# Stick-breaking attention: six projection k-steps moved from the first pair to the last two, and the next pair's sums and root one step later

## The reference

```
qkv = rmsnorm(x) @ w_qkv                 # 1024 x 3072
q, k = rmsnorm(q, q_gain), rmsnorm(k, k_gain)       # per head, over 64
z = q @ k.T / sqrt(64)
log_stay = where(s < t, log_sigmoid(-z), 0)
log_between = reverse_cumsum(log_stay) - log_stay
weights = where(s < t, exp(log_sigmoid(z) + log_between), 0)
x = x + (weights @ v) @ w_o
```

## Time and profile before

| | us |
|---|---|
| median of three runs | 1882.72 |
| the profiled execution's own time | 1882.4 |
| its span | 1880.6 |
| TensorE busy | 1848.2 (98%) |
| VectorE, ScalarE, GpSimd busy | 1034.4, 853.3, 1088.0 |

### The profile page before, as it was taken

The page is one execution under the profiler, slowest core; times in us unless marked ns, Lnnn a source line. Parts: engine busy times, 40 slices in busy tenths (PEclk is TensorE's granted clock), DMA queues, the critical chain, the costliest instruction groups (busy, mean ns, idle before and its releaser), DMA issues.

```text
span 1880.6 us, 28216 instructions
## 1 busy us (share of the span) xinstructions
PE 1848.2 (98%) x10422; PEld 1564.7 (83%) x10422; DVE 1034.4 (55%) x1863; ACT 853.3 (45%) x1562; POOL 1088.0 (58%) x1321
## 2 busy tenths in 40 slices
PE   8999999999999999999999999999999999999998
PEld 6888777888888878877899899878888888999997
DVE  5657664521223377775755555375755476555552
ACT  4565455532233356564544444344433354444341
POOL 5437333455556433325788888654433178888882
PEclk9999999999999999999999999999999999999999
DMA  6114222133333212212233333332222133333331
GB/s 193 60 45 124 57 56 58 51 84 101 98 95 115 86 57 68 57 46 78 85 99 107 105 91 112 101 98 82 68 68 57 46 101 101 102 101 102 101 101 56
DMA packets 269162, 160.42 MB, mean 85 GB/s; under 512 B 6137, under 2 KB 267489, under 8 KB 268898
## 3 DMA queue, kind: packets, MB, share of 16 engines
q1 hardware_dynamic: 269026, 158.61, 29.2%
HBM read 156.50 MB, written 2.10 MB: 84 GB/s over the span
## 4 chain that ended last, share of the span: by engine, by line
PE 90%; DVE 4%; ACT 3%; issue 2%; POOL 1%; DMA 0%; ACTq 0%; DVEq 0%; SPq 0%
PE bank L259 19%; PE bank L2025 13%; PE bank L622 7%; PE bank L624 7%; PE bank L623 7%; PE bank L2670 3%; PE bank L2672 3%; PE bank L2671 3%; PE bank L1617 2%; PE bank L424 2%; PE bank L1619 2%; PE bank L1618 2%; PE bank L426 2%; PE bank L425 2%; PE bank L802 1%
## 5 line engine op out<-in xcount | busy, mean ns | idle before, releaser
L241 POOL TENSOR_TENSOR weight_lo<-weight_stage,weight_hi 128x256 fp32r<-128x256 f32 x1160 | 965.5, 866 | 741.5 <-ACT weight_hi L229 741.5
L229 ACT ACTIVATE weight_hi<-weight_stage 128x1024 fp32r<-128x1024 f32 (+2 forms) x303 | 309.1, 1021 | 247.8 <-PE bank L259 180.3
L622 PE MATMUL bank<-a_hi,weight_lo 128*128 128x512 f32 (+1 forms) x464 | 197.9, 426 | 1.7 <-POOL weight_lo L241 1.4
L259 PE MATMUL bank<-hidden_lo,weight_hi 128*128 128x512 f32 x512 | 199.5, 390 | 0.0
L259 PE MATMUL bank<-hidden_hi,weight_lo 128*128 128x512 f32 x512 | 199.5, 390 | 0.0
L259 PE MATMUL bank<-hidden_hi,weight_hi 128*128 128x512 f32 x512 | 199.2, 389 | 0.0
L624 PE MATMUL bank<-a_hi,weight_hi 128*128 128x512 f32 (+1 forms) x464 | 182.7, 394 | 0.0
L623 PE MATMUL bank<-a_lo_rounded,weight_hi 128*128 128x512 f32 (+1 forms) x464 | 182.5, 393 | 0.0
L1991 POOL TENSOR_TENSOR block_weight_lo<-block_weight,block_weight_hi 128x256 fp32r<-128x256 f32 x156 | 124.7, 831 | 22.8 <-ACT block_weight_hi L2160 22.8
L2375 DVE TENSOR_TENSOR x_t<-x_t,bank 128x512 f32<-128x512 f32 x128 | 82.0, 677 | 90.4 <-PE bank L259 90.4
L259 PEld LDWEIGHTS bank<-hidden_hi,weight_hi 128*128 128x128 f32 x512 | 96.1, 188 | 20.2
(11 more groups left out here) (397 smaller groups left out, 4343.2 us busy)
## 6 DMA issues: line engine op xcount, KB each, us to landing
weight_stage<-in_mlp_w SPq DMA_DIRECT2D x128, 512.0 KB, 3.8
weight_stage<-in_w_in SPq DMA_DIRECT2D x57, 512.0 KB, 3.7
weight_stage<-in_hg_w_in SPq DMA_DIRECT2D x32, 512.0 KB, 3.9
weight_stage<-in_sb_w_qkv SPq DMA_DIRECT2D x24, 512.0 KB, 3.6
weight_stage<-in_w_mkv SPq DMA_DIRECT2D x8, 512.0 KB, 3.9
weight_stage<-in_w_out SPq DMA_DIRECT2D x8, 512.0 KB, 3.8
weight_stage<-in_sb_w_o SPq DMA_DIRECT2D x8, 512.0 KB, 3.8
weight_stage<-in_hg_w_o SPq DMA_DIRECT2D x8, 512.0 KB, 3.8
```

Of the source, the lines that this page charges most:

```text
L229: act.activation(self.hi[slot][:, 0:size], self.stage[slot][:, 0:size], ACT.Copy).then_inc(self.hi_done, 1)
L241: last = pool.tensor_tensor(self.lo[slot][:, part], self.stage[slot][:, part], self.hi[slot][:, part].bitcast(F32), ALU.subtract)
L259: last = pe.matmul(out, l, r, start=n == 0, stop=n == 3 * len(pairs) - 1)
L622: pe.matmul(to, wlo, ahi(k), start=k == 0, stop=False)
```

## The change

The number of k-steps per step is given by `share(m)`. The total stays at 208 calls in and before the loop. In the first pair steps have 4, 5, 4 and 5 (before: 6 each), steps 24 to 29 have 4 (before: 3), steps 30 and 31 stay at 3. The first portion of a step now comes ahead of `spread_k`. `sums` and `root` of the next pair move from step i=0 to i=1, `evict_q` with them; `evict_k` moves from step i=3 to step i=0 of the next pair; `evict_v` from i=1 to i=2 (in pair 6 it stays at i=3).

```diff
+            def share(m):
+                if m < NT:
+                    return 2, 2 + m % 2
+                if m < M - 2 * NT:
+                    return 3, 3
+                return (2, 2) if m < M - 2 else (1, 2) if m == M - 2 else (2, 1)
...
             for m in range(M):
                 p, i = divmod(m, NT)
                 more = p + 1 < PAIRS
+                some, rest = share(m)
+                fill(some)
                 if i == 2 and more:
                     spread_k(p + 1)
-                some = 3 if p + 2 < PAIRS else 2 if i % 2 else 1
-                fill(some)
                 if m >= 1:
                     turn(2 * m - 2)
                     turn(2 * m - 1)
...
                 if i % 2 and m >= 3:
                     weigh(m - 3)
                     weigh(m - 2)
-                fill(3 if some == 3 else 3 - some)
-                if i == 0 and more:
+                fill(rest)
+                if i == 1 and more:
                     sums(p + 1, 0)
                     sums(p + 1, 1)
...
                 weigh(2 * m + 1)
-                if i == 0 and more:
+                if i == 1 and more:
                     root(p + 1)
...
                 if i == 0 and p >= 1:
                     keep_v(p)
-                if i == 0 and more:
+                if i == 0 and more and p >= 1:
+                    evict_k(p + 1)
+                if i == 1 and more:
                     evict_q(p + 1)
                 if i == 2 and p >= 1:
                     put(p - 1)
-                if more and i == (1 if p + 2 < PAIRS else 3):
+                if more and i == (2 if p + 2 < PAIRS else 3):
                     evict_v(p + 1)
-                if i == 3 and p + 2 < PAIRS:
-                    evict_k(p + 2)
```

## The result

The changed kernel took 1895.43 us, the median of four runs (1893.43 to 1897.79), against 1882.36 us for the kernel before (four runs, 1881.57 to 1885.38). The ratio is 1.0066 with a 95% interval of 1.0053 to 1.0078: 0.66% slower, by 13 us. The profiled execution, the quickest of the four, took 1893.43 us, its span is 1891.6 us. TensorE's busy time is 1849.0 us, against 1848.2 before; what grew is its idle time.

The account below looks back on a forecast made before the run. TensorE, busy 98% of the span, was taken as the bound, so middle-pair pauses cost in full. Terms 10.6 + 4.5 + 2.3 - 3.4 = +14.0 us on 1882.4 gave 1896.5 us predicted; forecast 1892.5 to 1900 (66%), range 1889 to 1905.

Parts of the forecast that it names:

- Part 1: At spread_k in pairs 0 to 6, TensorE waits for VectorE's later root: 10.6 us lost together.
- the length of the root: VectorE's root between sums and spread_k takes 3.07 us when GpSimd's burst is over, 4.49 if they collide.
- the burst would be over before the root: In step i=1, GpSimd's weight-splitting burst ends by t0+6.2, before the root starts at t0+6.9 (t0: the step's turn).
- Rival A: Root and GpSimd's burst still collide, each root takes 4.49 us: +9.9 us, 1906 us; chance 13%.
- Part 2: Evicting k behind keep_v in step i=0 holds v's unit 0.9 us in five pairs: 4.5 us; step 25 adds 2.3.
- the score of step i=1 waits right behind: Without the eviction's pause, TensorE would stop about 0.8 us at step i=1's score for ScalarE's sigmoids.
- Rival B: One of a pair's two pauses is hidden: 1892 us without the eviction's, 1890 without the root's; chance 14%.
- Step 25's score: In pair 6, TensorE reaches this score early and waits for the sigmoids: 2.3 us lost.
- Part 3: In the last two pairs, extra k-steps remove or shrink four pauses: 3.4 us gained; two others stay.
- moving six k-steps costs nothing: Moving k-steps from pair 0 to steps 24 to 29 adds no work; pair 0 loses 0 us, bounds 0 and 1.
- Rival D: No change in time: new pauses equal those removed, 0.5 us a pair in place of 2.1; chance 4%.
- C: Faster: all six pauses in the last two pairs close and nothing new appears, 1876.5 us; chance 3%.

Follow-up runs that it names:

- e1: The changed kernel with spread_k moved behind the turn and score of step i=2 instead of ahead of them; 1888.30 us.
- e2: The changed kernel with evict_k put back in step i=3 of the pair before; 1888.15 us.
- e3: The changed kernel with both edits, spread_k behind turn and score and evict_k back in step i=3; 1881.84 us.
- e4: The changed kernel with evict_k ahead of keep_v instead of behind it in step i=0; 1894.88 us.
- e6: The changed kernel's k-steps with the old order of sums, root and evictions (in pair 6 sums, root and evict_q stay in i=1); 1882.60 us.
- e7: e6 with spread_k moved behind turn and score; 1882.34 us.
- e5: The kernel before with sums and root one step later and the first k-steps ahead of spread_k, evictions and k-step counts unchanged; 1896.78 us.
- e8: e3 with the last pair's turn_v ahead of the second portion of k-steps in step 28; 1878.77 us.

## Why the prediction was right

The forecast was 1896.5 us, and 1895.43 was measured. The mechanism was right: both kinds of new wait stand where they were forecast, as often as they were forecast, and e1, e2 and e3 show that removing them gives the time back. That the median came within 1.1 us is in part luck. The sum was +14.0 us, the stage of the profiled execution grew by 11.4, and that execution took 1893.43 us where the sum said 1896.4.

- Part 1, root: mechanism and places right, all seven waits at `spread_k` are there, and e1 shows that they are paid in full, but for what came back elsewhere. The size was too high: 7.0 us (0.81 x 5 + 1.5 x 2) in place of 10.6. The mis-sized term is the length of the root: I took 3.07 us from the earlier trace rows as the quick one, but that root still had one operation beside GpSimd's burst (0.49 us for 0.18); with none it is 2.75. The root of the earlier trace rows had a fourth one too (0.46 us), beside the three counted. The hand-over was 0.05 us (691.87 to 691.92), not 0.14, which had been read between ScalarE and TensorE. Pair 0 was forecast with one slow operation (2.5 us) and had none.
- That the burst would be over before the root: right, with 1.1 us to spare in the middle pairs. Rival A (1906) did not occur.
- Part 2, the eviction: 0.93 us x 5, as forecast (0.9). That the score of step i=1 waits right behind was shown by e4: 0.76 us in its place. Rival B, one of the two pauses hidden, did not occur.
- Step 25's score: 2.3 forecast, 2.2 in the bracket.
- Part 3: the pauses at `sums(7)` and in step 26 went, that at the turn of step 28 went too, those of 1.08 and 1.74 us stayed. The gain was forecast at 3.4. The brackets of the pauses that went make 3.05; measured over both pairs it comes to 3.3 (below).
- That moving six k-steps costs nothing: right for the five middle pairs (e6), and nearly so for pair 0. There e6 takes 3.6 us less than before, where six k-steps of 0.69 us make 4.1, so 0.5 us were lost, within the bounds of 0 and 1. Rival D would have needed new pauses no larger than those removed, and C fails as it was put: the root would have had to take 1.8 us.

The stage can be divided at turns, with the k-steps that were moved counted at 0.69 us each. From its start to the turn of step 4 it grew by 1.6 us, for which the forecast had 2.5. From there to the turn of step 24 it took 135.08 us before (679.01 to 814.09) and 145.18 after (676.18 to 821.36), 9.4 us more without the one k-step moved into it, for a forecast of 10.7. The last two pairs cost 0.4 us, for a forecast of 0.8; as their two new pauses make 1.5 + 2.2, the gain there was 3.3. The terms with these sizes, 7.0 + 4.7 + 2.2 - 3.3 = 10.6, leave 0.8 us of the stage's 11.4. Most of that lies in the five middle pairs: such a pair grew by 1.86 us, and its two losses make 1.74. What the rest is stays open.

## What to carry to other kernels

Where one engine is full, an order of work is judged by distances: from the instruction that starts a chain on another engine to the one that needs its end, in the full engine's own work, against the chain's length. Here 3.87 us of matmuls stood against a chain of 4.7 us, and that there would be a loss could be read off before it was built, though its size was read too high. Work that is moved away (the 1.74 us of `sums` in step i=0) may have been the cover of a third chain; and a wait that is removed often has a twin behind it (e4, e7), so look for the next one before counting the gain.

## What the runs showed of the hardware

A pause of TensorE can be followed by a stretch at a lower clock, and then costs more than its own length. In four of the ten profiled executions of changed kernels (e2 to e5) the granted clock fell within this stage, each time less than 1 us behind the end of a pause of 1.74 to 2.18 us. In e3 it was the one of 1.74 us that ended at 848.02; the stretches from 846 to 858 us (last three columns: clock, DMA share, GB/s):

```profile
846.00:850.00 4.00, 2.26 (x7) 1.60 (x6) 3.93 (x6) 2.17 (x4) 0.00 (x0) 0.77 0.00 0
850.00:854.00 4.00, 4.00 (x27) 3.15 (x26) 1.65 (x2) 0.90 (x2) 0.00 (x0) 0.81 0.00 0
854.00:858.00 4.00, 4.00 (x35) 3.27 (x35) 0.00 (x0) 1.09 (x2) 0.00 (x0) 1.00 0.00 0
```

In e4 it was the 2.18 us ahead of the score of step 25, and the 28 small matmuls behind took 3.26 us, where they take 1.75 in e1:

```profile
826.80 0.92 PE L1667 MATMUL bank<-sb_k,sb_q 64*128 64x256 f32 x8 [2.18 <-ACT sb_beta L1892]
827.66 3.26 PE L1692 MATMUL bank<-scratch,sb_v_tok 128*64 128x128 f32 x28
```

The granted clock is 0.50 from 827.70 to 831.00: the lower of the clock's two levels, 1.2 GHz in place of 2.4, at a price of about 1.5 us. The same pauses stand in the kernel before (1.74 us), in the change, in e1 and in e6 to e8 without it, so it does not always follow. That the pause is its cause is not shown.

This explains two numbers. From one step i=1 to the next, e4 takes 29.00 us and the change 29.16, 0.8 us less over five pairs, and still e4's stage is 0.8 us longer (282.29 against 281.50), because its last part holds this stretch. And the step from e3 to e8 (2.7 us of stage) holds e3's stretch, 1.6 us, beside the 1.16 us for the wait.

Other stages have such stretches too. At 138 us TensorE waits 1.23 us in the kernel before and in the change alike; before, the clock is down behind it, and in the change it is not (the first line is before, the second after):

```profile
138.00:142.00 4.00, 4.00 (x22) 4.00 (x23) 3.90 (x7) 0.40 (x1) 4.00 (x5) 0.58 0.45 131
138.00:142.00 4.00, 4.00 (x38) 4.00 (x37) 3.93 (x6) 1.27 (x3) 4.00 (x5) 1.00 0.43 131
```

In all nine experiments it is down there as well. Thus the change's profiled execution has the mean clock 0.999 because this stretch is missing. Its other three runs had 0.996 and 0.997 and took 1.1 to 4.4 us longer; where in them the clock fell is not on record, so this is likely, but not shown, to be what separates the median from the profiled execution. If it is, it is also why the median lies nearer to the forecast than the stage does.

The sentence of the prediction that pauses of this size cost their own length only was read from one execution, and it is not safe. In e8, which has the smallest sum of pauses (3.2 us), eight of ten runs had a mean clock of 0.998. Of the 20 runs of the kernel before beside it, nine had 0.996 or 0.997 and took 1882.9 to 1885.1 us, the others 1880.2 to 1882.9. Which executions get such stretches was not settled.
